# A decoder step's compression stage: the position bias as a column of the prompt's products, the first sample's keys begun in the prompt's compression, the second sample's chunks loaded during the projection

## The reference, cut to what matters

```python
def nsa_compress(kv, w_ck1, w_ck2, w_cv1, w_cv2, pe_k, pe_v):
    B, N = kv.shape[:2]
    n_chunks = N // CMP_STRIDE                   # chunks of 16 tokens
    n_cmp = n_chunks - CMP_RATIO + 1             # blocks of two chunks: 31 for the prompt, 127 for a sample
    ch = kv[:, :n_chunks * CMP_STRIDE].reshape(B, n_chunks, CMP_STRIDE, 2, NSA_KV_HEADS, HEAD_DIM)
    blocks = jnp.concatenate([ch[:, j:j + n_cmp] for j in range(CMP_RATIO)], axis=2)

    def mlp(x, pe, w1, w2):
        x = (x + pe[None, None, :, None, :]).transpose(0, 3, 1, 2, 4).reshape(B, NSA_KV_HEADS, n_cmp, CMP_BLK * HEAD_DIM)
        return jax.nn.silu(x @ w1) @ w2
...
def sb_attend(q, k, v, q_pos, k_pos):
    z = jnp.einsum('bqhd,bshd->bhqs', q.astype(jnp.float32), k.astype(jnp.float32)) / math.sqrt(HEAD_DIM)
```

## Time and profile before

| | |
|---|---|
| median of 3 executions | 1187.35 us (1182.03 to 1191.99) |
| the profiled execution's own time | 1191.54 us |
| its span, first to last instruction | 1189.7 us |
| PE busy in the span | 91% |
| compression stage, first to last product of it | 199.95 to 454.2 us |

### The profile page before, as it was taken

How to read it: one execution, slowest core, us unless ns; L and a number is a source line. 1 busy time by engine, 2 the same in 40 slices (tenths; PEclk the granted TensorE clock), 3 DMA queues, 4 the chain that set the end, 5 groups by cost and what they waited for, 6 DMA issues and landing times.

```text
span 1189.7 us, 23077 instructions
## 1 busy us (share of the span) xinstructions
PE 1084.4 (91%) x8348; PEld 953.0 (80%) x8348; DVE 617.1 (52%) x1042; ACT 392.6 (33%) x725; POOL 69.9 (6%) x83
## 2 busy tenths in 40 slices
PE   3996999998989998989999898999999999999993
PEld 2996999887878886555555557999999999999993
DVE  4431673586778787765444436445543335553332
ACT  4120212333333335556444435332231112221223
POOL 2000001221112100000000000110000000000002
PEclk9998997798999896988999978999999999999997
DMA  7529218799999963256666651323333333332321
GB/s 248 178 79 222 79 40 230 188 241 246 268 265 275 273 209 115 90 187 202 212 200 205 212 177 36 89 71 88 88 106 89 94 85 89 94 97 72 90 71 72
DMA packets 180131, 177.61 MB, mean 149 GB/s; under 512 B 13063, under 2 KB 140676, under 8 KB 177700
## 3 DMA queue, kind: packets, MB, share of 16 engines
q1 hardware_dynamic: 178610, 171.33, 50.7%
q10 hardware_dynamic: 1458, 5.43, 1.4%
HBM read 170.83 MB, written 10.06 MB: 152 GB/s over the span
## 4 chain that ended last, share of the span: by engine, by line
PE 64%; SPq 18%; issue 6%; DMA 4%; DVE 3%; ACT 3%; POOL 0%; POOLq 0%; DVEq 0%; ACTq 0%
PE bank L662 59%; SPq L576 4%; PE bank L666 4%; SPq L498 3%; SPq L540 2%; SPq L564 2%; SPq L543 2%; SPq L491 2%; DMA low_arena<-in_cache_nsa_slc_kv_dram 1%; DMA low_arena<-in_consts_dram 1%; DMA high_arena<-in_cache_sb_kv_dram 1%; DMA high_arena<-in_w_in_dram 1%; ACT low_arena L1550 1%; SPq L504 0%; SPq L582 0%
## 5 line engine op out<-in xcount | busy, mean ns | idle before, releaser
L662 PE MATMUL bank<-high_arena 128*128 128x254 f32 (+8 forms) x1864 | 239.6, 346 | 16.5 <-DMA high_arena<-in_cache_sb_kv_dram 6.6
L662 PEld LDWEIGHTS bank<-high_arena 128*128 128x128 f32 (+5 forms) x1864 | 185.2, 152 | 53.6 <-issue 10.1
L2114 DVE TENSOR_TENSOR w_low<-high_arena,w_high 128x1024 fp32r<-128x1024 f32 x72 | 90.1, 1252 | 84.1 <-ACT w_high L1487 74.2
L666 PE MATMUL bank<-low_arena 128*128 128x128 f32 (+3 forms) x658 | 108.0, 309 | 28.0 <-DMA page_ids<-in_page_table_dram 14.7
L666 PEld LDWEIGHTS bank<-low_arena 128*128 128x128 f32 (+3 forms) x658 | 87.4, 164 | 39.6 <-issue 27.2
L1487 ACT ACTIVATE w_high<-high_arena 128x1024 fp32r<-128x1024 f32 x72 | 76.3, 1060 | 114.8 <-PE bank L662 113.8
L662 PE MATMUL bank<-a_high,w_high 128*128 128x256 f32 (+1 forms) x512 | 104.3, 285 | 5.3 <-issue 2.9
L662 PE MATMUL bank<-h_high,w_high 128*128 128x256 f32 (+1 forms) x512 | 103.1, 283 | 1.8 <-DVE h_low L2141 1.8
L662 PE MATMUL bank<-a_low,w_high 128*128 128x256 f32 (+1 forms) x512 | 103.8, 284 | 0.0
L662 PE MATMUL bank<-a_high,w_low 128*128 128x256 f32 (+1 forms) x512 | 103.5, 283 | 0.0
L662 PE MATMUL bank<-h_low,w_high 128*128 128x256 f32 (+1 forms) x512 | 103.3, 283 | 0.0
(11 more groups left out here) (218 smaller groups left out, 1583.6 us busy)
## 6 DMA issues: line engine op xcount, KB each, us to landing
low_arena<-in_cache_sb_kv_dram SPq DMA_DIRECT2D x128, 256.0 KB, 4.9
high_arena<-in_cache_sb_kv_dram SPq DMA_DIRECT2D x128, 256.0 KB, 3.7
high_arena<-in_cache_nsa_cmp_kv_dram SPq DMA_DIRECT2D x128, 128.0 KB, 5.2
high_arena<-in_w_up_dram SPq DMA_DIRECT2D x32, 512.0 KB, 4.1
high_arena<-in_w_down_dram SPq DMA_DIRECT2D x32, 512.0 KB, 4.2
high_arena<-in_w_in_dram SPq DMA_DIRECT2D x10, 1136.0 KB, 5.6
low_arena<-in_cache_nsa_slc_kv_dram SPq DMA_DIRECT2D x128, 64.0 KB
high_arena<-in_cache_nsa_slc_kv_dram SPq DMA_DIRECT2D x128, 64.0 KB, 2.4
```

What stands on the lines that cost most here:

```text
L662: return T.matmul(out, lhsT=l, rhs=r, start=start, stop=stop, **k)
L666: return T.transpose(out, in_, ident[0:n, 0:n])
L2114: V.tensor_tensor(w_lo_r[u], w_raw[u], w_hi[u], ALU.subtract).then_inc(sem(f"w_lo{u}"), 1)
```

## The change

It does these things:

- **Bias.** The 32 one-column products and PE's and ACT's wait for them go. DVE writes the two halves of the position vector as two further columns behind the prompt's 32 chunks in `xT` (one copy for keys, one for values, before the transposes of queries and keys are evicted), and the prompt's hidden products run over 33 blocks for each head in place of 31 (66 columns for 62). Column 32 of the result is the bias. DVE takes it from there in `bias(kv)`, two instructions for each of `kv` 0 and 1, for which ACT's `sigmoid` now waits.
- **Keys of sample 0.** The first three of the six pieces of sample 0's key work are done in the prompt's compression; sample 0's own call does the other three, and has three empty `between()`. DVE does pages 0 to 6 of sample 0 around `bias` and `silu` of the prompt.
- **Loads.** Sample 1's 16 chunk loads are issued in the projection, after the last weight columns. For sample 0 SP then has keys alone to load, and it no longer waits for `snew` (a DVE result) before all of them but only before the ring's place 7. The prompt's own chunks are read back to another place (`nat_p`).
- The samples 0 and 1 are written out ahead of the loop, which has three turns.

The core of the diff:

```diff
@@ SP
             load_columns(*COLUMNS[1])
+            sp.wait_ge(sem("z_mm"), 5 * NCB // 2)
+            for half in range(2):
+                load_chunks(page_ids(NPG + 8 * half), 1, half)
...
+                        if p == 7:
+                            sp.wait_ge(sem("snew"), 2)
                         sp.wait_ge(sem(f"ring_free{p}"), i * 4 + 2 * u + half + 1)
...
-            sp.wait_ge(sem("snew"), 2)
-
-            with sp.Fori(0, 3) as i:
+
+            load_keys(0, 0, False)
+            load_keys(0, 1, True)
+            with sp.Fori(1, 3) as i:
@@ PE
-            for kv in range(2):
-                for m in range(16):
-                    ins = mm(bank[6][:, kv:kv + 1], w1[kv][:, m, :], vcol[:, 24 + 16 * kv + m:25 + 16 * kv + m],
-                             m == 0, m == 15)
-            ins.then_inc(sem("start_pe"), 1)
...
-            pe.wait_ge(*signal("pebias", 2))
+            pe.wait_ge(*signal("pe_cols", 1))
...
+            todo = key_work(0, 0)
+            compress(0, 1, next_of(todo, 3))
+            todo[2:2] = [lambda: None] * 3
+            compress(0, 2, next_of(todo))
+            compress(1, 2, next_of(key_work(0, 1)))
+            with pe.Fori(1, 4) as i:
@@ ACT
-            act.wait_ge(*signal("pebias", 2))
...
+                    if tiles == 1:
+                        act.wait_ge(*signal("pebias", kv + 1))
@@ DVE
+            for kv in range(2):
+                ins = V.tensor_copy(xT[kv][:, :, :, NCP + 1:NCP + 3],
+                                    over(vcol[:, 24 + 16 * kv:40 + 16 * kv].rearrange("p (two m) -> p m two", two=2), 2, KVH))
+            ins.then_inc(sem("start_dve"), 1)
...
+            def bias(kv):
+                dve.wait_ge(sem(f"hid_mm{kv}"), 1)
+                col = bank[2 + kv][:, NCP + 1:NCP + 2]
+                chain(V.tensor_copy(pebias[:, kv:kv + 1], col))
+                V.tensor_scalar(pebias[:, 2 + kv:3 + kv], col, -1.0, None, ALU.mult).then_inc(sem("start_dve"), 1)
...
+            sb_keys(0, 0, 0, 2)
+            bias(0)
+            sb_keys(0, 0, 2, 4)
             silu(0, 0, NCP + 1)
+            sb_keys(0, 0, 4, 5)
+            bias(1)
+            sb_keys(0, 0, 5, 7)
             silu(0, 1, NCP + 1)
             compressed_out(0, kc[:, B, 0:NCP], vc[0:NCP, B, :], NCP + 1)
+            sample_work(0, 0, 7)
+            sample_work(0, 1)
```

More of the change, by code:

```diff
@@ L202, in __enter__ @@
         self.first = c.n
-        self.loop = c.eng.Fori(0, self.count)
+        c.n = self.base = c.n - self.start * self.per
+        self.loop = c.eng.Fori(self.start, self.start + self.count)
         i = self.loop.__enter__()
@@ L777, in compress @@
                 nb = n - 1 if tiles == 2 else NCP
+                nh = nb if tiles == 2 else NCP + 2
                 past = int(tiles == 2)
```

105 lines of the change are left out of this document (57 added, 48 removed).

## The result

The changed kernel takes 1197.82 us in the median of 13 runs (1188.93 to 1203.83), the kernel before 1185.14 us in 13 runs beside it (1178.09 to 1192.14). The ratio is 1.0103, with a 95% interval of 1.0074 to 1.0131: some 12 us slower, where 2.5 us were predicted. The forecast of 1190 was wrong, and so was its range, 1179 to 1197: the median lies just beyond its upper end, for which the prediction's chance of a loss over 1% was 0.04.

What follows compares the result with a forecast made beforehand. The stage's end was taken to move with SP reaching sample 1's second-half quad (256.82), if PE is not later. Ring and PE put that at 259.3 to 259.4, 2.5 us later: 1187.35 + 2.5, say 1190; range 1179 to 1197.

Steps and rivals of the forecast that it cites:

- The loop's unrolling: SP's loop over the samples: writing out turns costs nothing, between -0.5 and +1 us.
- SP needs 156.8 us: SP's queue from sample 1's second-half quad to sample 6's window: 156.8 us, with no wait worth the name.
- The key work: Prompt's compression: two more quads and two sets of scores add 5.4 us; sample 0 starts 4.7 us later.
- ACT's copy as what remains late: Start of the prompt's compression: PE's second chunk transposes wait for it until 198.2; of 10.6 us saved, 3.0 remain.
- the half clock until past 224: Prompt's compression on PE: granted clock 0.50 from 194 to past 224.
- DVE's bias and pages ahead of the second `silu`: End of the prompt's compression: these and the second layer put 4.2 us before sample 0's start at 224.0.
- sample 0 itself: PE: 15.3 us to the end of its keys' hidden products at 239.3; sample 1 starts near 251.6.
- DVE's order: Samples 0 and 1: silu ahead of pages 8 to 13 holds SP's ring; the quad goes out at 259.3 to 259.4.
- the trace leaned against the page: Clock rise at 224.2 after 16 transposes: transposes seem to count as work, unlike the skill's rule; only one such rise.
- first rival: Prompt's compression: the clock comes back to full, all moves forward by 8.6 us, giving 1181; chance 16 in 100.
- second rival: Sample 1: the ring does not hold SP because DVE is further on, giving 1183; chance 8 in 100.
- the third: Projection: sample 1's chunk loads delay the last weight columns, PE 4.6 us late, 1194.5; chance 13 in 100, other delays included.

Runs made afterwards that it cites:

- e11: The change without its key work, SP's loop fully written out, ACT's small transfers where they were; against the kernel before: 0.998.
- e5: The changed kernel with the rest of SP's loop written out too, so without a jump; against the kernel before: 1.0048.
- e2: The kernel before with only SP's first two samples written out ahead of its loop; against the kernel before: 1.0045.
- e4: The change without the key work: bias part, chunk loads in the projection, SP's first two samples written out; against the kernel before: 1.005.
- e14: e5 with sample 0's last two full pieces of key work two places later; against the kernel before: 1.0009.
- e13: e5 with all of DVE's pages 7 to 15 of sample 0 ahead of both silu; against the kernel before: 1.0024.
- e16: The change with SP's loop written out, pages 7 to 15 ahead of both silu, key pieces later, ACT's transfers late; against the kernel before: 0.9971.
- e9: The change without key work, SP's loop written out, ACT's six small transfers behind the prompt's compression; against the kernel before: 0.9933.
- e10: The kernel before with the bias part and ACT's six small transfers behind the prompt's compression; against the kernel before: 0.996.
- e3: The kernel before with sample 1's chunk loads in the projection and SP's first two samples written out; against the kernel before: 1.0042.
- e6: The changed kernel with DVE's pages 8 to 13 of sample 0 ahead of the first silu; against the kernel before: 1.0102.
- e7: The changed kernel with ACT's six small transfers moved behind the prompt's compression; against the kernel before: 1.0126.
- e15: The change with only sample 0 of SP's loads written out ahead of a loop of three turns; against the kernel before: 1.0151.
- e17: The changed kernel with 78 already-met SP waits added, which moved SP's loop by 39 instructions; against the kernel before: 1.0155.
- e1: The kernel before with the bias part of the change alone; against the kernel before: 1.0001.
- e12: The kernel before with sample 0 alone written out ahead of SP's loop, which keeps three turns; against the kernel before: 0.9997.
- e18: The kernel before with 50 already-met SP waits added, which moved SP's loop by 25 instructions; against the kernel before: 1.0.

## Why the prediction was wrong

In medians the 12 us come together like this: bias, loads and a loop without jumps -0.2% (e11), the key work +0.7% (e5 over e11), the stall at the jump +0.55% (after over e5; e2 alone shows +0.45%). Each term carries 0.4 to 0.5% of uncertainty, and the three add up by the way they are formed. Taken in the other order, the jump is +0.7% (e4 over e11) and the key work +0.5% (after over e4). Both causes are shown; how the loss divides between them is known only roughly.

**The step that failed** is the term "The loop's unrolling I cost at nothing, between -0.5 and +1: before shows no gap when a loop starts, and nothing there bounds it better". It looked at the loop's start. What costs is the loop's jump back. Before jumps twice, and a gap with a jump in it is some 0.5 us longer than one without; the changed kernel jumps once and loses 3.4 us in the profiled execution. e2, which has only this edit, loses 5.9 us at the jump and 0.45%; e5, without any jump, has no gap and half the loss. With it falls the sentence that SP needs 156.8 us from sample 1's quad to sample 6's window: it needed 163.9, 3.2 of the difference at the jump and the rest in slower issues, for which no run shows a cause.

**The second cause had the right sign and a wrong size.** The key work was to cost 4.7 us at the start of sample 0 (measured 5.1, of which 1.1 came before it), and of these 2.5 were to be left at SP's quad (measured 5.2). The parts of the first number held: ACT's copy as what remains late, so that little of the bias part's 10.6 us is kept; the half clock until past 224; DVE's bias and pages ahead of the second `silu`. The term that was mis-sized is sample 0 itself, and in it the part behind the keys' hidden products: up to their end it took 15.7 us (predicted 15.3), from there to sample 1 it took 16.0 (predicted 12.3, before 15.0). The prediction let PE start sample 1 near 251.6, 27.6 us after sample 0; it took 31.7. It counted the pieces of key work as work at full clock only, and "the three pieces saved would have come partly here and partly behind". They were also what PE did while ACT made copies: e14 moves the two that are left beside ACT's work and gains 3.0 us, of which 1.7 are idle time. In the changed kernel the part behind the keys' hidden products has 12 transposes and 24 score records fewer than before, worth some 3.7 us by before's rows; the waits took back 3.3, and the last 16 score records, at half clock, 1.4 (3.37 us for 2.01).

**DVE's order** was predicted to hold SP in sample 1, from the first `silu` at 240.8 (measured 241.79) on, with the second at 250.3 (measured 252.47, now waiting for PE's products and ACT, not for the pages). SP did wait for DVE there. But as a cause it does not carry: with that wait gone, in e13, SP waits for PE instead and nothing is won by the window of sample 1.

**The rivals.** The clock did not come back in the prompt's compression: granted 0.50 from 200 to 225, with eight of the twelve quad transposes in that stretch and four ahead of it, from 196.93. The prediction held that the trace leaned against the page and that transposes might count as work for the clock. The Trainium skill (TensorE: Matmul & The Clock Gate, Part 4: PE-mode transpose) says that they do not. This stretch is what that sentence gives, but it decides little, since the two quads in it fill 1.7 of the 25 us. e16 leans the other way, as the earlier trace rows did: PE was idle for 2.9 us, did a second layer of four records from 223.17 and twelve transposes from 223.74, and the clock was back when the next product began at 226.74:

```profile
225.00:227.00 2.00, 1.84 (x9) 0.54 0.32 91
227.00:229.00 2.00, 2.00 (x11) 1.00 0.91 287
```

(PE alone: busy time and records, granted clock, DMA share, GB/s.) So the first rival did not come, but whether transposes count for the clock stays open. The ring did hold SP, so the second rival fell. The chunk loads did not delay the weight columns, so the third fell too, though the side on which it lay was the right one.

**Why the medians and not the profiled total.** The two profiled executions differ by -1.8 us while the medians differ by +12.7. Had only these been compared, the change would pass for a small gain.

**What stays open** is what makes the jump dear in one program and cheap in another. What is shown: code is fetched at the dear jumps (one or two packets inside each gap) and not at the cheap ones, and without a jump there is no gap. That the fetch is what SP waits for is the likely reading; no run varies it alone. The loop's length hardly differs (332 to 338 instructions). All cases seen fit a bound on the loop's end: 435, 460 and 587 have no stall, 593, 735, 743 and 782 have one. They fit a count of blocks as well. The Trainium skill (Runtime: NRT & Kernel Launch, Instruction fetch mechanics) says that a taken branch to a target outside the window of two blocks that the engine holds waits for the fetch of that block. The prediction did not weigh this sentence, though it names the cost that came; the trace agrees with it in kind, and does not show why the same loop pays nothing in before. The refills of 16 KiB that the same section states appear on one of the two instruction queues only; on the queue with the packets of the dear jumps a packet has half of that. The page of the profile of before lists both:

```profile
q8 instruction: 40, 0.66, 0.2%
q14 instruction: 23, 0.19, 0.1%
```

That is 16 KB and 8 KB a packet. Also open is how what e16 loses against e9 ahead of sample 0 divides between the half clock and the wait of 3.9 us for the first quad.

## What to carry to other kernels

Writing out a few turns ahead of a loop on a queue that sets the pace is an edit with a price of its own: look for a gap of issue at the loop's line and for instruction packets in it, and if it is there, write the loop out altogether (e5), or keep it whole. Before work is moved to an earlier stage, ask what it did where it was: small pieces that stood in another engine's latency cost little there, and leave holes when they go; and work moved from a stretch at full clock to one at half clock takes about twice its time (a set of scores 1.56 us for 0.81 in the changed kernel). And when a saving at one place ends at a wait for another engine's transfers (here ACT's six small ones), move those first; that alone made the bias part worth 0.4% (e10), and with the loads and SP's loop written out 0.7% (e9; the step from e10 to e9 is within the noise).

## What was not expected of the hardware

- The step from a window to the next query row over a jump back of SP took 4.2 to 7.2 us in eight programs (after, e2, e3, e4, e6, e7, e15, e17), and 1.1 to 1.2 us in five (before, e1, e10, e12, e18), with nearly the same loop; without a jump it takes 0.5 to 0.9, and once 1.2 (e13). The nearest pair is e12, whose loop ends at instruction 587, and e15, where it ends at 593; they also differ by the rest of the change, so that the six instructions are not shown to be what decides.
- One such jump cost 0.45 to 0.7% of the time, 5 to 8 us, with intervals of about 0.4% on each; the gap alone is 3 to 6 us longer than a cheap one. PE did not make up for it: its waits for quads were 16.8 us in place of 11.4, and 10.3 in e5, which has no jump.
- The last scores of sample 0 ran mostly at half clock in the changed kernel, e5 and e14 (3.37 us and twice 3.50 for 16 records) and at full clock in e9 and e16 (2.01 us for the same), after the same wait of about 2 us in e16 as in e14. Its first 16 hidden products took 5.19 us in the changed kernel, 4.72 in e14, 3.64 in e16, and 5.67 in e9, which has no key work in the prompt's compression. A mean clock read from one stage of one execution does not carry over to the next variant.
